# A decoder of four layers: the start and the gate projections reordered, and two ring slots per transfer in the expert-choice layers

## The reference

```python
def first_block(x, c, positions, ...):            # layers 0 and 1
    cos, sin = _rope_tables(positions)
    c_act = jax.nn.silu(c)
    for i in range(DEPTH):
        mod = c_act @ ada_w[i] + ada_b[i]
        sh1, sc1, g1, sh2, sc2, g2 = jnp.split(mod[:, None, :], 6, axis=-1)
        h = _rmsnorm(x, norm_g[i, 0]) * (1.0 + sc1) + sh1
        ...                                        # mixer, then hier_moe

def expert_choice_moe(x, router_w, w1, w3, w2):   # layers 2 and 3
    aff = jax.nn.softmax(jnp.einsum('bsd,de->bse', x, router_w).astype(jnp.float32), axis=-1)
    gates, idx = lax.top_k(aff.transpose(0, 2, 1), cap)          # cap = 32
    xg = jax.vmap(lambda xb, ib: xb[ib])(x, idx)
    hid = jax.nn.silu(jnp.einsum('becd,edf->becf', xg, w1)) * jnp.einsum('becd,edf->becf', xg, w3)
    ye = jnp.einsum('becf,efd->becd', hid, w2) * gates[..., None].astype(x.dtype)
    ...                                            # scattered back and added

# second_block, after the mixer of a layer
ffn = expert_choice_moe(x, router_w[i], w1[i], w3[i], w2[i])
ple = jax.nn.sigmoid(x @ ple_gate_w[i] + ple_gate_b[i]) * (p[i] @ ple_w[i])
x = layer_norm(DEEPNORM_ALPHA * x + ffn + ple, ln2_g[i], ln2_b[i])
```

## Time and profile before

| | |
|---|---|
| median of 3 runs | 2327.95 us (2327.0 to 2330.36) |
| the profiled execution | 2323.29 us, of it the span from first to last instruction 2321.5 us |
| TensorE busy | 1823.3 us, 79% of the span |
| VectorE, ScalarE busy | 419.2 us, 383.5 us |
| mean granted TensorE clock | 0.879 of full speed |
| bytes moved by DMA | 716.03 MB, mean 308 GB/s |
| the first expert-choice layer, first up block to last down block | 1180.95 to 1646.8 us |
| the second one | 1826.90 to 2292.0 us |

### The profile page before, as it was taken

The page is one execution under the profiler, slowest core; times in us unless marked ns, Lnnn a source line. Parts: engine busy times, 40 slices in busy tenths (PEclk is TensorE's granted clock), DMA queues, the critical chain, the costliest instruction groups (busy, mean ns, idle before and its releaser), DMA issues.

```text
span 2321.5 us, 30494 instructions
## 1 busy us (share of the span) xinstructions
PE 1823.3 (79%) x13099; PEld 1136.1 (49%) x13099; DVE 419.2 (18%) x946; ACT 383.5 (17%) x813; POOL 0.6 (0%) x5
## 2 busy tenths in 40 slices
PE   5989898889898998899978656666789786656565
PEld 4867655558566655486746121221477452212112
DVE  2232311122533111123311000000143210000001
ACT  3031210121533110223311000000223210000001
POOL 0000000000000000000000000000000000000000
PEclk8999799999898999999989787877899897777868
DMA  9768399984563999933469999999933699999994
GB/s 358 231 235 315 150 387 393 395 254 155 224 224 136 362 389 390 336 112 141 164 254 341 422 421 421 421 421 421 340 138 110 237 345 420 421 421 421 422 421 166
DMA packets 183900, 716.03 MB, mean 308 GB/s; under 512 B 27692, under 2 KB 95192, under 8 KB 113240
## 3 DMA queue, kind: packets, MB, share of 16 engines
q1 hardware_dynamic: 183052, 712.29, 78.7%
q10 hardware_dynamic: 716, 1.81, 0.2%
HBM read 826.25 MB, written 1.05 MB: 356 GB/s over the span
## 4 chain that ended last, share of the span: by engine, by line
PE 56%; DMA 32%; DVE 5%; SPq 3%; ACT 2%; issue 2%; ACTq 0%; POOLq 0%; DVEq 0%
DMA ring<-in_w 26%; PE ps L915 19%; PE ps L1298 7%; DMA ring<-in_moe_w_up 6%; PE ps L1223 6%; PE ps L1308 3%; PE ps L1209 3%; PE ps L1233 2%; PE ps L1250 2%; PE ps L898 2%; PE ps L1016 2%; PE ps L980 1%; SPq L753 1%; PE ps L1152 1%; PE ps L927 1%
## 5 line engine op out<-in xcount | busy, mean ns | idle before, releaser
L1298 PE MATMUL ps<-ring,ptb 128*32 128x512 f32 x1936 | 327.4, 827 | 212.0 <-DMA ring<-in_w 196.6
L1298 PEld LDWEIGHTS ps<-ring,ptb 128*32 128x32 f32 x1936 | 85.4, 145 | 443.0 <-issue 440.8
L1308 PE MATMUL ps<-ring,pb 128*32 128x512 f32 x1024 | 144.9, 720 | 87.7 <-DMA ring<-in_w 85.0
L915 PE MATMUL ps<-xT,ring 128*128 128x256 f32 (+2 forms) x640 | 149.8, 396 | 7.6 <-ACT xT L1599 3.8
L915 PEld LDWEIGHTS ps<-xT,ring 128*128 128x128 f32 (+2 forms) x640 | 120.5, 191 | 33.7 <-issue 12.6
L1308 PEld LDWEIGHTS ps<-ring,pb 128*32 128x32 f32 x1024 | 39.5, 129 | 187.4 <-issue 183.5
L915 PE MATMUL ps<-oT,ring 128*128 128x256 f32 x512 | 112.8, 380 | 2.7 <-DVE oT L1950 1.6
L915 PE MATMUL ps<-hT,ring 128*128 128x256 f32 x480 | 108.4, 384 | 5.3 <-ACT hT L1593 5.3
L2213 DVE TENSOR_TENSOR kT<-pb,ps 128x1024 f32<-128x1024 f32 x8 | 9.8, 1221 | 535.7 <-ACT pb L1746 535.7
L1223 PE MATMUL ps<-ring,yT 128*32 128x256 f32 x1536 | 92.2, 398 | 18.2 <-DMA ring<-in_moe_w_up 17.0
L915 PEld LDWEIGHTS ps<-oT,ring 128*128 128x128 f32 x512 | 97.0, 190 | 16.8 <-DVE oT L2002 2.0
(11 more groups left out here) (408 smaller groups left out, 1921.5 us busy)
## 6 DMA issues: line engine op xcount, KB each, us to landing
ring<-in_w SPq DMA_DIRECT2D x370, 1024.0 KB
ring<-in_moe_w_gate SPq DMA_DIRECT2D x96, 1024.0 KB
ring<-in_moe_w_up SPq DMA_DIRECT2D x96, 1024.0 KB
ring<-in_moe_w_down SPq DMA_DIRECT2D x96, 1024.0 KB
ring<-in_ada_w SPq DMA_DIRECT2D x48, 1024.0 KB
ring<-in_diff_w_in SPq DMA_DIRECT2D x12, 1024.0 KB
ring<-in_w_o SPq DMA_DIRECT2D x8, 1024.0 KB
ring<-in_ple_gate_w SPq DMA_DIRECT2D x8, 1024.0 KB
```

Source lines behind the costliest of these rows:

```text
L915: last = mmul(o, l, r, start=start, stop=stop)
L1298: last = mmul(ps[32 * j:32 * j + 32, 2 * a + h, :], xg[:, k, 32 * j:32 * j + 32], w[j][2 * k2 + h], start=(k == 0), stop=(k == C - 1))
L1308: last = mmul(ps[32 * j:32 * j + 32, 6 + h, :], hidT2[:, c, 32 * j:32 * j + 32], w[j][2 * c2 + h], start=(c == 0), stop=(c == C - 1))
```

## The change

It has three parts.

1. **The start.** The constants are cut in two: 513 columns (identity, ones, mean, before, inv_freq) come first, the rest (`consts_rest`) goes to SyncE's queue behind the first two projection slots, and the first rope waits for it. Positions and lambda have a semaphore of their own (`others`). On ScalarE the Squares follow the copies of x directly, the Sqrt follows the Silu, and the Sin goes behind `gain(0)`. TensorE does the norm's sums before the parameter columns, and lambda behind the ada products. VectorE does lambda first, and the norm's scaling before it waits for lambda.
2. **The gate projections** of the expert-choice layers are spread over group 0: one each behind the second, third and fourth block of up products, and one behind the transposes. Their slots stand at 16, 24 and 32 (two) of the order. They use PSUM bank 7 and each waits for the evacuation of the one before.
3. **The expert slots.** Two neighbouring slots of a matrix are one DMA with rows of 16 KB, wherever they don't wrap around the ring's end. `landed[n]` holds semaphore and value for each slot. The blocks of `gate_up` and `down` take eight slots, two per expert: wait for all eight, 32 matmuls (16 waves of records), and the last four matmuls free two slots each. The transfers of a pair wait for the release of the slot that the second one replaces.

```diff
-N_PARAMS, N_LATE = 21, 20
+N_FIRST = CONST["ones64"][0]
+N_PARAMS, N_LATE = 19, 20
...
+        GATE_AT = (16, 24, 32, 32)
+        GATE_BANK = 7
+        e2_slot = {}
         def moe2_slots(layer):
             ph[f"value{layer}"] = len(jobs)
             ple_value_jobs(layer)
-            up_slots[layer] = n_slot[0]
-            n_slot[0] += 32 - len(GUESTS)
             ph[f"gate{layer}"] = len(jobs)
-            ple_gate_jobs(layer, range(4))
-            rest_slots[layer] = n_slot[0]
-            n_slot[0] += 16 + 48 * (E2_GROUPS - 1)
+            for i, x in itertools.product(range(E2_GROUPS), range(48)):
+                if i == 0:
+                    ple_gate_jobs(layer, [a for a in range(4) if GATE_AT[a] == x])
+                if i or x not in GUESTS:
+                    e2_slot[layer, i, x] = n_slot[0]
+                    n_slot[0] += 1
...
+        def signal(n, slots=1):
+            signals[n % RING] += 1
+            for x in range(slots):
+                landed[n + x] = S(f"slot{n % RING}"), 16 * signals[n % RING]
+            return S(f"slot{n % RING}")
...
                 def expert_slots(i, ss):
-                    for s in ss:
-                        n = slot2(l, i, s)
-                        load(n, ring[:, n % RING, :], rows(i, s))
+                    ss = list(ss)
+                    while ss:
+                        s, n = ss[0], e2_slot[l, i, ss[0]]
+                        if s % 2 == 0 and s + 1 in ss and n % RING < RING - 1:
+                            w, j, kk = order[s]
+                            sp.wait_ge(S("slot_used"), n + 1 - RING + 1)
+                            sp.dma_start(ring[:, n % RING:n % RING + 2, :].rearrange("p s n -> p (s n)"),
+                                         w[l, 4 * i + j][:, SLOT * kk:SLOT * kk + 2 * SLOT]).then_inc(signal(n, 2), 16)
+                            ss = ss[2:]
+                        else:
+                            load(n, ring[:, n % RING, :], rows(i, s))
+                            ss = ss[1:]
...
             load_ada(range(ADA_FIRST))
-            load_jobs(span["diff"][:4])
+            load_jobs(span["diff"][:2])
+            sp.dma_start(cst[:, N_FIRST:N_CONST], A["consts"][:, N_FIRST:N_CONST]).then_inc(S("consts_rest"), 16)
+            load_jobs(span["diff"][2:4])
...
                 def gate_up(i):
-                    for kk in range(4):
+                    for kk in range(2):
                         for a in range(2):
-                            s = 8 * kk + 4 * a
-                            w = [slot_of(i, s + j) for j in range(4)]
-                            for k2, h, j in itertools.product(range(2), range(2), range(4)):
-                                k = 2 * kk + k2
+                            s = 16 * kk + 8 * a
+                            w = [slot_of(i, s + x) for x in range(8)]
+                            for x, k2, h, j in itertools.product(range(2), range(2), range(2), range(4)):
+                                k = 4 * kk + 2 * x + k2
                                 last = mmul(ps[32 * j:32 * j + 32, 2 * a + h, :], xg[:, k, 32 * j:32 * j + 32],
-                                            w[j][2 * k2 + h], start=(k == 0), stop=(k == C - 1))
-                                if k2 and h and not (i == 0 and s + j in GUESTS):
-                                    last.then_inc(S("slot_used"), 1)
+                                            w[2 * j + x][2 * k2 + h], start=(k == 0), stop=(k == C - 1))
+                                held = [y for y in (s + 2 * j, s + 2 * j + 1) if not (i == 0 and y in GUESTS)]
+                                if x and k2 and h and held:
+                                    last.then_inc(S("slot_used"), len(held))
+                            if i == 0 and kk + a:
+                                project(span[f"gate{l}"][2 * kk + a - 1:2 * kk + a])
...
                     last.then_inc(S("hT_mm"), 1)
+                    if i == 0:
+                        project(span[f"gate{l}"][3:])
                     pe.wait_ge(S("hidT_ready"), n)
...
                     if i == 0:
-                        project(span[f"gate{l}"])
+                        await_need(pe, ("job", span[f"gate{l}"][-1]))
...
             last.then_inc(S("xT_mm"), 1)
+            norm(0)
             pe.wait_ge(S("params"), 16 * N_PARAMS)
...
-            pe.wait_ge(S("lam_ready"), 1)
-            mmul(ps[:, 7, 0:1], K("ones", 1), misc[0:1, 8:9], start=True, stop=True).then_inc(S("lam_mm"), 1)
-            norm(0)
...
-            act.dma_start(cst[:, :], A["consts"]).then_inc(S("consts"), 16)
+            act.dma_start(cst[:, 0:N_FIRST], A["consts"][:, 0:N_FIRST]).then_inc(S("consts"), 16)
...
+            squares(0)
             act.wait_ge(S("cols_mm"), 1)
...
+            std(0)
             act.wait_ge(S("lam_sum"), 1)
             func(misc[0:1, 4:6], misc[0:1, 2:4], ACT.Exp).then_inc(S("lam_exp"), 1)
+            act.wait_ge(S("slot_used"), 4 * ADA_FIRST)
+            func(ada_rows01, ps[:, 0, :], ACT.Copy).then_inc(S("ada_evac"), 1)
+            gain(0)
             act.wait_ge(S("ang_ready"), 1)
```

More of the change, by code:

```diff
@@ L50, in _layout @@
     at = 0
[L51 to L52 removed]
+    for name, n in (("ident", P), ("ones", P), ("mean", P), ("before", P), ("inv_freq", 1),
+                    ("ones64", P), ("rot64", P), ("rot_mla", P), ("tri_f", P), ("tri_b", P), ("iota", P), ("slots", 3 * P), ("rot16", P),
                     ("slot_col", E1_GROUPS), ("spill", E1), ("first", E1), ("bump", E1), ("limits", T // BLK), ("pair", E1_GROUPS // 2),
                     ("cos_m", T), ("sin_m", T), ("cos_g", T), ("sin_g", T),
[L55 removed]
+                    ("fold", 2 * NCMP), ("cmp_ok", TT * NCMP), ("cmp_bd", 2)):
         CONST[name] = (at, n)
@@ L282, in ada_view, with job @@
             return ring[:, n % RING, :].rearrange("p (k n) -> p k n", k=2)
-        def job(W, k, cols, mm, evac, new=True, last=True, need=None, eng="act"):
+        def job(W, k, cols, mm, evac, new=True, last=True, need=None, eng="act", bank=None):
             if new:
@@ L287, in job @@
             jobs.append(dict(W=W, k=k, cols=cols, mm=mm, evac=evac, new=new, last=last,
-                             slot=n_slot[0] - 1, need=need, eng=eng, n=len(jobs)))
+                             slot=n_slot[0] - 1, need=need, eng=eng, n=len(jobs),
+                             bank=len(jobs) % 2 if bank is None else bank))
             return len(jobs) - 1
@@ L801, in fixed @@
                     sp.wait_ge(S("slot_used"), n - RING + 1)
-                    sp.dma_start(ring[:, n % RING, :], srcs[w][m, E1_FIXED[j]]).then_inc(S(f"slot{n % RING}"), 16)
+                    sp.dma_start(ring[:, n % RING, :], srcs[w][m, E1_FIXED[j]]).then_inc(signal(n), 16)
                 def block_at(g, j):
@@ L811, in routed @@
                     sp.wait_ge(S("slot_used"), n - RING + 1)
-                    sp.dma_start(ring[:, n % RING, :], srcs[w][m, e], cond=on > 0).then_inc(S(f"slot{n % RING}"), 16)
+                    sp.dma_start(ring[:, n % RING, :], srcs[w][m, e], cond=on > 0).then_inc(signal(n), 16)
                 for s in range(12):
@@ L894, in slot_in @@
             def slot_in(n):
-                pe.wait_ge(S(f"slot{n % RING}"), 16 * (n // RING + 1))
+                pe.wait_ge(*landed[n])
             def tr(dst, src, k=P):
@@ L907, in project @@
                         slot_in(jb["slot"])
-                    if j >= 2:
+                    if jb["bank"] == GATE_BANK:
+                        if jobs[j - 1]["bank"] == GATE_BANK:
+                            await_need(pe, ("job", j - 1))
+                    elif j >= 2:
                         await_need(pe, ("job", j - 2))
-                    for x, grp in enumerate(jb["mm"](slot_view(jb["slot"], jb["k"], jb["cols"]), j % 2)):
+                    for x, grp in enumerate(jb["mm"](slot_view(jb["slot"], jb["k"], jb["cols"]), jb["bank"])):
                         for i, (o, l, r, *flags) in enumerate(grp):
@@ L1308, in down @@
                             last = mmul(ps[32 * j:32 * j + 32, 6 + h, :], hidT2[:, c, 32 * j:32 * j + 32],
-                                        w[j][2 * c2 + h], start=(c == 0), stop=(c == C - 1))
-                            if c2 and h:
-                                last.then_inc(S("slot_used"), 1)
+                                        w[2 * j + x][2 * c2 + h], start=(c == 0), stop=(c == C - 1))
+                            if x and c2 and h:
+                                last.then_inc(S("slot_used"), 2)
@@ L1340, in experts2 @@
                             pe.wait_ge(S(f"Y_ready{c // 4}"), n)
-                        if i == 0 and c == 0:
-                            await_need(pe, ("job", span[f"gate{l}"][-1]))
                         b = c // 2 if i < E2_GROUPS - 1 else last_bank(c // 2)
@@ L1446, in _ @@
             last.then_inc(S("modT_mm"), 1)
+            pe.wait_ge(S("lam_ready"), 1)
```

(5 more changed lines are left out.)

91 lines of the change are left out of this document (46 added, 45 removed).

## The result

The changed kernel takes 2380.72 us (median of 4 runs, 2376.64 to 2385.86), against 2327.47 us of the kernel before in the same session (4 runs, 2321.81 to 2330.36): ratio 1.0233, 95% interval 1.0202 to 1.0264. It is slower by 53 us; the prediction was 2382. The profiled execution took 2385.86 us, with a span of 2384.1.

The account below looks back on a forecast made before the run. Expert-choice layers were taken as bound by their weight loads. Per layer 37.6 + 3.5 + 4.0 - 6.4 - 8.4 = +30.3, both +61, start -7: +54 on 2323.3 us, 2377, adjusted to the median as 2382; range 2335 to 2412.

Parts of the forecast that it names:

- Stalls, 37.6 us per layer: Expert-choice layers: each of 16 cold eight-slot blocks per layer stalls the weight stream by 2.35 us, 37.6 us per layer.
- landing: Expert-slot loads: delay beyond transfer time until restarted slots have landed, taken as 2.0 us, between 0.5 and 2.7.
- way: From the end of a block, which frees its slots, to the restart of the weight stream: 1.05 us.
- First release, +3.5: Start of an expert-choice layer: TensorE frees the first slots after eight rather than four, 3.5 us later.
- Last block, +4.0: End of an expert-choice layer: the block behind the last landing takes 9.1 us instead of 5.06, +4.0.
- Gate projections, -8.4 per layer: Group 0 of expert-choice layers: spread projections remove both stream gaps, 8.4 us less per layer on average.
- Rows of 16 KB, -6.4 per layer: Expert-slot transfers: 428 instead of 421 GB/s saves 0.04 us on about 160 paired slots, 6.4 us per layer.
- Rival (d): Expert-slot transfers: 16 KB rows are no faster, 8 us above the main case, 2390; a quarter of its 0.68 chance.
- The start, -7: Kernel start: first projection at 33.5 instead of 42.3 us; net 7 us less, between 4 and 10.
- (b): Expert blocks: TensorE stays at 2.4 GHz, 7.0 us per block, landing under 1.75; 26 us faster, 2302. Chance 0.12.
- (c): Expert blocks: stalls near their lower bound, 1 us each; 10 us slower, 2338. Chance 0.12.
- (e): Expert blocks: clock rises later or engines' lag grows, 5 us per stall; 138 us slower, 2466. Chance 0.08.

Follow-up runs that it names:

- Experiment 3: The changed kernel with blocks of eight slots, but every slot a transfer of its own with 8 KB rows: 2381.06 us, ratio 1.0255.
- 4: The changed kernel with every second expert product left out, transfers, waits and slots as they are: 2303.19 us, ratio 0.9915.
- 6: Both reorderings, single transfers; TensorE waits for eight slots but frees four half way and four at the end: 2308.81 us, ratio 0.9931.
- 7: Both reorderings, single transfers; TensorE waits for four slots at a time but frees eight after every second block: 2305.58 us, ratio 0.9925.
- experiment 10: The changed kernel run again, unaltered, on the same chip as experiments 8 and 9: 2378.1 us, ratio 1.0248 to the kernel before.
- experiment 1: New start and spread gate projections only; expert slots as in the kernel before (blocks of four, single transfers): 2295.52 us, ratio 0.9883.
- experiment 5: The changed kernel with pairs and 16 KB rows, but blocks of four slots, two experts at a time: 2311.9 us, ratio 0.9944.
- experiment 2: The new start alone: experiment 1 with the gate projections back in one piece, as before: 2312.19 us, ratio 0.9959.
- experiment 8: Half of the expert products left out, as in experiment 4, but every slot a single transfer with 8 KB rows: 2301.23 us, ratio 0.9908.
- experiment 9: The changed kernel with 13 unused constant products behind each of the first three up blocks of groups 1 to 3: 2364.33 us, ratio 1.0185.

## Why the prediction was right

The mechanism was right: the stream of weights runs dry behind nearly every block of eight, since only four of the twelve slots are on their way meanwhile (0 GB/s in the window from 1325 to 1327). Experiment 3 shows that it is the block and not the pair, 4 that it is the time for which it is held, 6 and 7 that it needs the wait for eight and the late release together. Term by term:

- **Stalls, 37.6 us per layer.** The interval behind a cold block was predicted at 19.6 + 2.35 = 21.95 and measured at 21.97 in the profiled execution, 21.72 in the first layer of experiment 10. Its parts: block 9.1 predicted, 9.04 measured; landing 2.0 predicted, and 12.93 - 1.05 - 9.8 = 2.1 measured, if the way is 1.05 and the rate as predicted. The count was a little off. The prediction let three first down blocks be warm behind a gather; the last group has no gather, and its block took 8.79. And a warm block did stall the stream: 1.3 us behind the one at 1510.69. The restart of the stream fits the way: SyncE issued behind the first release at 1179.84 (row below), next to nothing moved until 1181, and 249 GB/s in the 1.5 us behind it, where the earlier trace rows have 0 and 197.
- **First release, +3.5.** The first block and SyncE's first issue behind it are 1179.84 - 1172.76 = 7.08 us behind the start of the layer; before it was 3.65. +3.4. The timeline of SyncE's queue:

```profile
1179.84 0.38 SPq L761 DMA_DIRECT2D ring<-in_ple_gate_w  x1
```

- **Last block, +4.0.** It lasted 9.96 in the first layer (the row at 1664.24) against 5.22, +4.7, and 8.82 in the second against 5.06, +3.8. Experiment 6, which keeps this term alone, has +3.9 and +3.8, and experiment 7, which keeps the first release alone, +3.5 and +3.8.
- **The whole block of eight.** With single transfers each predicted stall is 0.15 shorter, so that the three terms give 2 x (37.6 - 16 x 0.15 + 3.5 + 4.0) = 85.4. Experiments 1 and 3 are 85.5 apart, and 82.1 of it lies in the layers; that the two agree to 0.1 is luck.
- **Gate projections, -8.4 per layer.** Experiments 1 and 2: -16.7 for both layers in the medians, -8.3 and -9.0 in the table. The timeline after has them one by one behind the up blocks, 7.2 us each:

```profile
1230.95 7.17 PE L940 MATMUL ps<-xT,ring 128*128 128x256 f32 x32
...
1239.14 7.14 PE L940 MATMUL ps<-xT,ring 128*128 128x256 f32 x32
```

- **Rows of 16 KB, -6.4 per layer.** This is the term that failed. The rate was right: the estimate was 428 GB/s, and experiment 5 shows 427 and 428 in its slices. The step "about 160 slots per layer travel in pairs: 160 x 0.04" took it for granted that a faster transfer makes a shorter interval also where the stream is waited for. There it doesn't: net of the longer stalls the pairs should have brought 2 x (6.4 - 2.4) = 8 us, and the changed kernel stands at 1.0233 and 1.0248 beside 1.0255 without pairs, 1.6 to 5 us, which the intervals don't tell from nothing. The intervals say the same: 21.69 and 21.65 us in the groups 1 to 3 of experiment 3, 21.77 and 21.81 in the changed kernel, 21.54 and 21.60 in its second run. Rival (d), 62 us over the kernel before, had this outcome with another reason, rows that are no faster; experiment 3, which has no pairs, came out at 58, the start being a little better. The Trainium skill ("DMA: Bandwidth & Descriptors", Why small descriptors are slow) counts about 3 cycles of overhead per packet beside one for each 32 bytes; worked out from that, an estimate, this step gains 0.6%. Experiment 5's 428 against 421 is 1.7%, so the measurement decides for the line through the rows.
- **The start, -7.** Measured -9.5, or -10.5 by the medians (experiment 2), at the better end of the range. The chain at the start after the change:

```profile
21.54 8.79 PE ps L1043 x128
...
33.04 14.41 PE ps L940 x64
```

The first projection at 33.04 was predicted at 33.5. In this execution it came by another path: I had the ada products wait for their weights, and they start at 21.54, when ScalarE has the Silu of c ready, and never wait for data. A window of their first 3 us (columns as above) has them at half clock instead:

```profile
21.50:24.50 3.00, 2.96 (x28) 1.39 (x32) 2.79 (x8) 2.97 (x3) 0.00 (x0) 0.50 1.03 416
```

That is why 128 records take 8.79 us where they took 7.09. But in another execution of the same kernel, experiment 10, the path is the predicted one. Its chain has the last ada weights landing at 30.08, where 29.5 was predicted, and the last products behind them:

```profile
6.57 23.51 DMA ring<-in_ada_w
...
30.12 1.11 PE ps L1043 x16
...
33.95 14.41 PE ps L940 x64
```

Of the eleven profiled executions with the new start, six (2, 4, 7, 8, 9, 10) wait for the ada weights, four (the changed kernel, 1, 3, 5) follow ScalarE's chain, and 6 waits for the weights of the first projection; the first projection stands between 32.8 and 35.2 in all of them. The 2 us that I had charged to the projections didn't come: two jobs take 14.41, as before. So the start now has two limits within a us or two of each other, the bytes ahead of the ada products and the chain of ScalarE ahead of the Silu, and to shorten one alone would bring little.

Put together by the runs: -27.2 for both reorderings (experiment 1), +85.5, and -2 to -5 for the pairs, is +53 to +57; measured +53 and +56.5. The direction and the size were earned, the last few us were not. The pairs brought 2 to 5 us where 8 were due, and this was made up for by a start 2.5 to 3.5 better; and two executions of the changed kernel differ by 9.5 us in their layers alone. So 2382 beside 2380.72 is luck. The rivals: (b), TensorE at 2.4 GHz and a short landing, fell with blocks of 8.3 to 10.0 us behind every long wait; experiment 9 shows that even with the clock held in nearly half of the blocks the kernel stays 1.85% slower. (c) fell with stalls of about 2 us. (e) fell too: the longest interval in the groups 1 to 3 of the changed kernel and of experiment 10 is 24.0 us, a stall of 4.4.

What stays open: why the wait from the end of a block to the next start varies between 12.2 and 15.4 us between two blocks of eight without a gate projection between them (the changed kernel, 3, 9 and 10), and why it is often longer than 12.5 us behind a warm block (13.7 to 14.1 us behind five of the eight in the first layer of experiment 9, 12.6 behind the other three). In experiment 8 the longer waits, up to 16.2 us, are no riddle: the blocks start about 19.9 us apart, at the pace of the stream, and a shorter block leaves more of that. Experiments 4 and 8 show that pairs make the intervals a little longer, not why.

## What to carry to other kernels

With a ring, count for each block what is still on its way while it is held: slots minus the slots held, times the transfer time of one, must exceed block + way to the queue + landing, here 9.8 against 12 us. A larger block that is waited for and given back as a whole takes from that budget twice; splitting either the wait or the release was enough here to be rid of all of the 41 us per layer but the 4 at its ends. Larger rows are worth their 1.7% only where the stream never waits, so check the budget first, and time the parts of a mixed change apart: here two of them brought 27 us and the third cost 81 to 85.

## What the runs showed of the hardware

A 16 KB row per packet took the stream from 421 to 428 GB/s (experiment 5). With 4 MB in flight when a block of eight ended and 4 MB more to come, the next block started 12.2 us after that end at best and 15.4 at worst (the changed kernel, experiments 3, 9 and 10, where no gate projection stands between), although 4 MB take 9.8. In the same runs TensorE came back to a block of eight at its full clock after every wait of up to 1.4 us. After waits of 2.2 to 3.0 us it did so in some cases (blocks of 7.07 us behind 2.23, 2.61 and 2.99) and came back at half of it in others (8.77 behind 2.30 and 2.48, 8.66 behind 2.77). Behind waits of 4.5 us and more every block took 8.3 to 10.0. And with the same bytes in flight, single transfers of 1 MB kept a steady 420 GB/s behind blocks of 3.6 to 6.6 us, where pairs of 2 MB fell to 416 (experiments 8 and 4).
